# A decoder step's indexer: sequences in pairs on two row halves and two column tiles, prompt scores over four PSUM banks

## The chip, the cores and the metric

The kernel runs on one core of one Trainium2 chip. The metric is device time in microseconds (us). Before the change it is 2095.02 us, the median of three runs (2094.37 to 2096.9).

## The reference, cut to what matters

One layer of a hybrid decoder serves a prompt of 272 rows (16 meta tokens and 256) and eight samples of eight rows each, 336 rows in all, with one set of weights. A combined projection makes queries, keys and values, the indexer's queries, keys and head weights, and the conv and gate inputs. The indexer scores every key for every query row, and only the best scored keys are attended to:

```python
def index_scores(iq, iw, ik, q_pos, k_pos):
    s = jnp.einsum('bqhd,bkd->bqhk', iq, ik).astype(jnp.float32) * (IDX_DIM ** -0.5)
    s = jnp.einsum('bqhk,bqh->bqk', jax.nn.relu(s), iw.astype(jnp.float32)) * (IDX_HEADS ** -0.5)
    return jnp.where(k_pos[None, None, :] <= q_pos[None, :, None], s, -jnp.inf)
```

There are 16 indexer heads of 64 values. A sample scores 1024 keys from a paged cache (8 pages of 128) and its 8 new ones, and takes the best 256; a prompt row scores up to 272 and takes 64. Attention, a conv branch, the gated merge and the feed-forward layer follow.

## The kernel before

**Weights.** The whole kernel is a stream of weight tiles of 2048 x 128. SyncE loads a tile into one of four slots of RAW (two transfers, released by `mm_done`). ScalarE makes its high part WH (`quarter`, line 558), VectorE the rest WL (line 949). TensorE multiplies each of the 16 weight blocks three times with 320 or 336 columns of activations (`split_mm`, lines 1416 to 1418). One such unit is cut into four quarters of 12 matmuls (`x_quarter`), which can be put between other work.

**Indexer keys.** GpSimd loads 64 pages (line 423). For each sequence b, ScalarE's `pages(b)` (line 599) copies the eight pages to `ikb` with the 64 values written twice, so that a key fills 128 rows. TensorE's `keys(b)` transposes eight blocks of it, and ScalarE and VectorE copy halves of the result to `ikTa` (lines 603 and 990). There are eight such sets: seven between the units of the stage "iq" (indexer queries) and one behind "ikiw" (keys and head weights).

**Indexer queries.** ScalarE evacuates each iq unit to `iqT` (prompt) and `iqs` (samples). In `iqs` the even heads lie in rows 0 to 63 and the odd ones in rows 64 to 127, in columns of their own, with zeros elsewhere (memset, line 985). One matmul of 128 rows so gives all 16 heads x 8 query rows of one sequence.

**Order on TensorE behind the ikiw unit.** The last set of keys; two quarters of the unit qk 0 (attention queries); small transposes and products that end with `d_setup` (line 1550 and on); the two other quarters of qk 0; then, sequence by sequence, `scores(b)` (two fp32 matmuls of 512 columns into SB or TB), relu on ScalarE (line 650) and VectorE (line 1027) to `rl`, and `total(b)` (two matmuls of 512 columns with the head weights IW, 64 columns wide, added up over all eight sequences in MB). Eight small matmuls score the new keys (`n_mm`), eight more sum them. VectorE copies the sums to Ss and Ws (lines 1032 to 1035).

**Prompt scores.** A loop of 32 steps (16 heads x 2 query tiles; in each four steps two with 144 and two with 272 keys): TensorE makes the scores of one head in a bank of SB (`i % 2`), with contraction over 64 rows, even heads in rows 0 to 63 and odd ones in rows 64 to 127; ScalarE's relu writes `rp` (line 657); VectorE multiplies it by the head's weight and adds it to Sp (lines 1042 and 1045). After each eight steps TensorE does a quarter of the unit qk 1. TensorE waits for the relu two steps back, ScalarE for the addition two steps back.

**Behind the loop.** ScalarE waits for all 32 additions, makes WH of the third unit of qk, and then squares the first unit; TensorE waits for that square (`squares(0)`, in the page `psM<-sq,ones`), and goes on with the third unit.

`ikT`, the new keys, exists in rows 0 to 63; GpSimd copies it to rows 64 to 127 by a transfer (line 435) once `ik_cp` has its four counts.

Of the kernel before, what the change touches and what calls it, by code (L numbers as in the profile page):

```python
# [31 lines left out]
P = 128  # L32
# [3 lines left out]
NS = B * Q  # L36
# [7 lines left out]
NPG = PAST // PAGE  # L44
LS = PAST + Q
# [81 lines left out]
def place(persistent, transient):  # L127
# [64 lines left out]
    ("ikst", [P, B, NPG, ID], F32, ST_A, ST_IKIW),  # L192
    ("iqT", [P, H, SEQ], F32, ST_IQ, ST_INDEX), ("iqs", [P, B, H, 2, Q], F32, ST_IQ, ST_INDEX),
# [3 lines left out]
    ("ikb", [P, 2, NPG, 2, ID], F32, ST_IQ, ST_IKIW), ("ikTa", [P, B, PAST], F32, ST_IQ, ST_INDEX),  # L197
    ("rl", [P, 2, PAST], F32, ST_INDEX, ST_INDEX), ("rln", [P, NS], F32, ST_INDEX, ST_INDEX), ("rp", [P, 2, NP], F32, ST_INDEX, ST_INDEX),
# [24 lines left out]
           "ut ML esel xs L ikst Tb OH vtok xTs crt ikb SGB m8p qsz ktok v2 oh relb relx m8s vst kst ya vT kTs iktok Lp CH "  # L223
# [3 lines left out]
def layer(nc, I, O):  # L227
# [44 lines left out]
    iktok, iwtok, ikb, ikTa, rl, rln, rp = (T[x] for x in ("iktok", "iwtok", "ikb", "ikTa", "rl", "rln", "rp"))  # L272
# [12 lines left out]

    def keys_of(qt):
        return N_META + P * (qt + 1)

    with ExitStack() as ctx:
        G, TB, SB, MB = ([ctx.enter_context(nc.psum_tensor(f"ps{n}{i}", [P, 512], F32)) for i in range(2)] for n in "GTSM")  # L290

# [12 lines left out]
        pool_init, pool_zero, pt_dn = sem("pool_init"), sem("pool_zero"), sem("pt_dn")  # L304
# [4 lines left out]
        pg_ld, d_setup, d_iw, d_ikt, d_page, ik_tr = sems("pg_ld", B), sem("d_setup"), sem("d_iw"), sem("d_ikt"), sem("d_page"), sem("ik_tr")  # L309
        n_mm, d_rln, ik_dp, ik_cp = sem("n_mm"), sem("d_rln"), sem("ik_dp"), sem("ik_cp")  # L310
# [90 lines left out]
        def _(pool):  # L401
# [13 lines left out]
            pool.tensor_copy(ptab2[:].rearrange("o (g n c) -> o g n c", g=B // 2, c=2), ptab[:].rearrange("o (g c n) -> o g n c", g=B // 2, c=2)).then_inc(pt_dn, 1)  # L415
            pool.wait_ge(pt_dn, 1)
# [4 lines left out]
            for b in range(B):  # L421
                for t in range(NPG):
                    pool.dma_start(ikst[:, b:b + 1, t, :], cache_ik[bass.ds(page(b * NPG + t), 1)].rearrange("o s d -> s o d")).then_inc(pg_ld[b], 16)
                if b == 0:
                    pool.wait_ge(a_rms, 1)
                    n = XTILES[2][1]
                    pool.tensor_scalar(xs[0:n, 2, :], xtok[0:n, 2, :], stat[0:n, 10:11], None, ALU.mult).then_inc(a_xp, 1)
                    for dst, src in ((oh[:], I["c_oh"]), (relx[0:BUCKETS, :], I["rel_bias"]), (wrow[:], I["w_dw"][0]),
                                     (esel[64:64 + IH, :], I["c_esel"]), (qm[:], I["c_qm"]), (cms[:], I["c_cms"]), (cmp_[:], I["c_cmp"])):
                        pool.dma_start(dst, src).then_inc(c2_ld, 16)  # L430
                if b == 1:
# [106 lines left out]
        def _(act):  # L538
# [62 lines left out]
            def keys(b):  # L601
                act.wait_ge(ik_tr, b + 1)
                act.activation(ikTa[:, b, 0:512], TB[0][:], ACT.Copy).then_inc(d_cpA, 1)

            def iq(g):
                for s in range(4):
                    u = 4 * g + s
                    if u >= 2:
                        keys(u - 2)
# [4 lines left out]
                    act.activation(iqT[:, u, :], G[s % 2][:, 0:SEQ], ACT.Copy)  # L614
                    for r in range(2):
                        rows = slice(64 * r, 64 * r + 64)
                        ins = act.activation(iqs[rows, :, u, r, :], G[s % 2][rows, SEQ:NQ].rearrange("p (b q) -> p b q", b=B), ACT.Copy)
                    ins.then_inc(ev[s % 2], 1)
                    pages(u)
# [9 lines left out]
            keys(6)  # L629
# [10 lines left out]
            keys(7)  # L640
# [7 lines left out]
            for b in range(B):  # L648
                act.wait_ge(idx_mm, b + 1)
                act.activation(rl[:, b % 2, 0:512], (SB, TB)[b % 2][0][:], ACT.Relu).then_inc(d_rlA, 1)  # L650
# [279 lines left out]
        def _(dve):  # L930
# [54 lines left out]
            dve.memset(iqs[:], 0.0)  # L985
            dve.memset(IW[:], 0.0).then_inc(pool_zero, 1)

            def keys(b):
                dve.wait_ge(ik_tr, b + 1)
                dve.tensor_copy(ikTa[:, b, 512:PAST], TB[1][:]).then_inc(d_cpD, 1)  # L990
# [11 lines left out]
            for u in range(4 * GN["iq"]):  # L1002
                if u >= 2:
                    keys(u - 2)
                if u == 3:
                    dve.wait_ge(c2_ld, 112)
# [4 lines left out]
            for s in range(4):  # L1011
                if s == 2:
                    keys(6)
                if s == 3:
                    keys(7)
# [9 lines left out]
            for b in range(B):  # L1025
                dve.wait_ge(idx_mm, b + 1)
                dve.tensor_scalar(rl[:, b % 2, 512:PAST], (SB, TB)[b % 2][1][:], 0.0, None, ALU.max).then_inc(d_rlD, 1)
            dve.wait_ge(n_mm, 1)
            dve.tensor_scalar(rln[:], SB[0][:, 0:NS], 0.0, None, ALU.max).then_inc(d_rln, 1)
            dve.wait_ge(sum_mm, B)  # L1030
            for i in range(2):
                dve.tensor_copy(Ss[:, 512 * i:512 * i + 512], MB[i][0:NS, :])
            dve.wait_ge(sum_mm, B + 1)
            ch.link(dve.tensor_tensor(Ss[:, PAST:LS], TB[0][0:NS, 0:Q], cms[:], ALU.min))
            dve.tensor_copy(Ws[:], Ss[:]).then_inc(d_ss, 1)

            for i in range(2 * IH):
# [3 lines left out]
                if h == 0:  # L1041
                    ins = dve.tensor_scalar(Sp[:, qt, 0:nk], rp[:, i % 2, 0:nk], iwtok[:, qt, h:h + 1], None, ALU.mult)
                else:
                    dve.wait_ge(pp_acc, i if i % 2 else i - 2)
                    ins = dve.scalar_tensor_tensor(Sp[:, qt, 0:nk], rp[:, i % 2, 0:nk], iwtok[:, qt, h:h + 1], Sp[:, qt, 0:nk],
# [361 lines left out]
        def _(pe):  # L1407
# [96 lines left out]
            def keys(b):  # L1504
                pe.wait_ge(d_page, b + 1)
                if b:
                    pe.wait_ge(d_cpA, b)
                    pe.wait_ge(d_cpD, b)
                for t in range(NPG):
                    ins = tr(TB[t // 4][:, P * (t % 4):P * (t % 4) + P], ikb[:, b % 2, t, :, :].rearrange("p r d -> p (r d)"))  # L1510
                ins.then_inc(ik_tr, 1)

            for u in range(4 * GN["iq"]):
# [4 lines left out]
                if u:  # L1518
                    keys(u - 1)
                if u == 3:  # L1520
                    pe.wait_ge(c2_ld, 112)
# [20 lines left out]
            keys(B - 1)  # L1542
# [3 lines left out]
            pe.wait_ge(d_cpA, B)  # L1546
            pe.wait_ge(d_cpD, B)
# [9 lines left out]
            for r in range(2, 4):  # L1557
# [420 lines left out]
```

## Time and profile before

| | |
|---|---|
| median of three runs | 2095.02 us |
| span of the profiled execution, first to last instruction | 2085.9 us |
| TensorE busy | 2031.4 us, 97% |
| VectorE busy | 1244.2 us, 60% |
| ScalarE busy | 888.5 us, 43% |
| GpSimd busy | 165.6 us, 8% |
| mean granted TensorE clock | 0.990 |
| HBM read, written | 338.91 MB, 10.83 MB |

The execution that was profiled is known by its span. The median of the runs lies 9.1 us above it, which is what lies around the first and the last instruction. A busy TensorE is one with a matmul in flight: the recorded length of a matmul holds its way through the array, so that records overlap, and the pitch from start to start tells what one costs.

### The profile page before, as it was taken

To read this page: it belongs to the slowest core of one execution; us is meant where nothing else is said; L and a number is where in the kernel's file an instruction comes from. 1 tells how busy PE (TensorE), PEld (TensorE's weight loads), DVE (VectorE), ACT (ScalarE), POOL (GpSimd) and SP (SyncE) were. 2 spreads that over 40 slices of the span, in tenths; PEclk is the share of its full clock that TensorE was granted. 3 is DMA by queue.
4 is the path that set the end of the run, shared out by engine and by line. 5 is a ranking of instruction groups with operands and counts; after the bars stand their busy time and mean duration, and the time that the engine had idled before them with its cause. 6 is when DMAs were issued, how large, how long until landed. Compare 5 with 4: busy or idle time off the path is not lost.

```text
span 2085.9 us, 40295 instructions
## 1 busy us (share of the span) xinstructions
PE 2031.4 (97%) x14517; PEld 1935.0 (93%) x14517; DVE 1244.2 (60%) x2293; ACT 888.5 (43%) x1640; POOL 165.6 (8%) x293
## 2 busy tenths in 40 slices
PE   6999999899999999999999999999999999999997
PEld 5957989899997778999999999999999999999997
DVE  5327997566667998955655555544455554455553
ACT  6424444343334333356444545533344433344443
POOL 6300000111113220010000000000000000000012
PEclk9999999999999999999999999999999999999999
DMA  9363454477768994556555555555555555555573
GB/s 240 94 127 106 128 134 130 135 227 236 237 203 291 333 323 129 147 152 197 149 154 142 157 144 147 155 142 156 146 151 150 145 157 141 156 147 152 150 204 109
DMA packets 545493, 350.54 MB, mean 168 GB/s; under 512 B 15122, under 2 KB 524346, under 8 KB 545007
## 3 DMA queue, kind: packets, MB, share of 16 engines
q1 hardware_dynamic: 518480, 263.55, 46.9%
q0 software_dynamic: 25824, 84.55, 12.5%
q8 instruction: 69, 1.13, 0.2%
q10 hardware_dynamic: 1088, 1.05, 0.2%
q14 instruction: 32, 0.26, 0.0%
HBM read 338.91 MB, written 10.83 MB: 168 GB/s over the span
## 4 chain that ended last, share of the span: by engine, by line
PE 68%; DVE 0%; ACT 0%; DMA 0%; issue 0%; POOL 0%; POOLq 0%; DVEq 0%; ACTq 0%
PE psG L1416 21%; PE psG L1417 21%; PE psG L1418 21%; PE psS L1413 2%; PE psM L1417 1%; PE psM L1418 1%; PE psM L1416 1%; PE psT L1410 0%; DMA vst<-in_cache_v 0%; PE psM L1410 0%; DVE OL L1285 0%; PE psM L1413 0%; PE psM L1774 0%; ACT WH L558 0%; POOL out L528 0%
## 5 line engine op out<-in xcount | busy, mean ns | idle before, releaser
L949 DVE TENSOR_TENSOR WL<-RAW,WH 128x512 fp32r<-128x512 f32 (+1 forms) x996 | 674.1, 691 | 624.4 <-ACT WH L558 622.5
L558 ACT ACTIVATE WH<-RAW 128x512 fp32r<-128x512 f32 (+1 forms) x996 | 613.8, 628 | 820.9 <-PE psG L1418 761.4
L1416 PE MATMUL psG<-XH,WH 128*128 128x320 f32 (+1 forms) x2688 | 852.8, 317 | 2.5 <-DVE WL L949 2.1
L1417 PE MATMUL psG<-XL,WH 128*128 128x320 f32 (+1 forms) x2688 | 838.5, 312 | 0.0
L1418 PE MATMUL psG<-XH,WL 128*128 128x320 f32 (+1 forms) x2688 | 836.9, 311 | 0.0
L1416 PEld LDWEIGHTS psG<-XH,WH 128*128 128x128 f32 x2688 | 507.4, 189 | 32.9 <-issue 25.0
L1417 PEld LDWEIGHTS psG<-XL,WH 128*128 128x128 f32 x2688 | 507.6, 189 | 1.6 <-issue 0.2
L1418 PEld LDWEIGHTS psG<-XH,WL 128*128 128x128 f32 x2688 | 507.5, 189 | 0.0
L1416 PE MATMUL psG<-MH,WH 128*128 128x320 f32 x960 | 297.9, 310 | 0.3 <-DVE ML L1385 0.3
L1418 PE MATMUL psG<-MH,WL 128*128 128x320 f32 x960 | 296.6, 309 | 0.0
L1417 PE MATMUL psG<-ML,WH 128*128 128x320 f32 x960 | 296.6, 309 | 0.0
L1416 PEld LDWEIGHTS psG<-MH,WH 128*128 128x128 f32 x960 | 180.5, 188 | 0.5 <-issue 0.5
L1417 PEld LDWEIGHTS psG<-ML,WH 128*128 128x128 f32 x960 | 180.5, 188 | 0.0
L1418 PEld LDWEIGHTS psG<-MH,WL 128*128 128x128 f32 x960 | 180.5, 188 | 0.0
L1249 DVE SCALAR_TENSOR_TENSOR ya<-ub,wdw,ya 128x256 f32<-128x256 f32 x232 | 99.9, 478 | 0.0
L527 POOL DMA_DIRECT2D out<-ytok x16 | 11.4, 712 | 1083.8 <-ACT ytok L909 1079.7
L1410 PE MATMUL psT<-ident,kst 128*128 128x128 f32 x512 | 68.9, 278 | 0.0
L1410 PEld LDWEIGHTS psT<-ident,kst 128*128 128x128 f32 x512 | 57.9, 142 | 6.8 <-issue 6.3
L759 ACT ACTIVATE kTs<-psT 128x512 f32<-128x512 f32 x64 | 38.2, 597 | 56.5 <-PE psT L1410 56.2
L1169 DVE COPY kTs<-psT 128x512 f32<-128x512 f32 x64 | 43.9, 686 | 25.3 <-PE psT L1410 25.3
L899 ACT ACTIVATE MH<-at 128x320 f32 x44 | 20.8, 472 | 83.0 <-DVE at L1383 83.0
L467 POOL DMA_DIRECT2D kst<-in_cache_k x64 | 33.9, 530 | 175.2 <-issue 175.2
(342 smaller groups left out, 1661.3 us busy)
## 6 DMA issues: line engine op xcount, KB each, us to landing
RAW<-in_w_in SPq DMA_DIRECT2D x160, 512.0 KB, 5.2
RAW<-in_w_ffn_down SPq DMA_DIRECT2D x96, 512.0 KB, 5.1
RAW<-in_w_ffn_gate SPq DMA_DIRECT2D x88, 512.0 KB, 4.8
RAW<-in_w_ffn_up SPq DMA_DIRECT2D x88, 512.0 KB, 4.7
kst<-in_cache_k POOLq DMA_DIRECT2D x64, 512.0 KB, 4.2
vst<-in_cache_v POOLq DMA_DIRECT2D x64, 512.0 KB, 6.0
RAW<-in_w_out SPq DMA_DIRECT2D x32, 512.0 KB, 4.7
RAW<-in_w_attn_br SPq DMA_DIRECT2D x16, 512.0 KB, 5.0
```

The lines of the kernel that those rows point to most:

```text
L467: pool.dma_start(dst[:, n:n + 1, :], src[bass.ds(page(g * m + n, ptab2), 1)].rearrange("o s n -> s o n")).then_inc(landed[n], 16)
L558: act.activation(WH[:, s % 2, 4 * r:4 * r + 4, c], RAW[:, s, 4 * r:4 * r + 4, c], ACT.Copy).then_inc(hi_done, 1)
L759: act.activation(kTs[:, j % 2, 0:4, :], TB[0][:].rearrange("p (h n) -> p h n", h=4), ACT.Copy).then_inc(kc_A, 1)
L899: act.activation(MH[:, bass.ds(g * 2 + s // 2, 1), :], at2[:, s // 2:s // 2 + 1, :], ACT.Copy).then_inc(ah_dn, 1)
L949: dve.tensor_tensor(WL[:, s, k, c], RAW[:, s, k, c], WH[:, s % 2, k, c].bitcast(F32), ALU.subtract).then_inc(lo_done, 1)
L1169: dve.tensor_copy(kTs[:, j % 2, 4:8, :], TB[1][:].rearrange("p (h n) -> p h n", h=4)).then_inc(kc_D, 1)
L1249: ch.step(dve.scalar_tensor_tensor(z, x, tap, z, ALU.mult, ALU.add))
L1410: return pe.transpose(out, src, ident[0:n, 0:n])
L1413: return pe.matmul(out, lhsT, rhs, start=start, stop=stop, skip_group_check=True)
L1416: pe.matmul(out, WH[:, s % 2, k], hi, start=start, stop=False)
L1417: pe.matmul(out, WH[:, s % 2, k], lo, start=False, stop=False)
L1418: return pe.matmul(out, WL[:, s, k], hi, start=False, stop=stop)
```

## The change

- `ikst` holds the pages of sequences p and p + 4 side by side, and their transposes give keys of p in rows 0 to 63 and of p + 4 in rows 64 to 127. The copy to `ikb` is gone; there are four sets of keys (behind units 2, 4, 6 and behind ikiw) instead of eight. GpSimd loads the sequences in the order 0, 4, 1, 5, ...
- `iqs` holds each sequence's 16 heads in its own row half. ScalarE writes the heads that lie in the right half at once and the others to `iqx`; two transfers on GpSimd's queue move these to the other half. The memset is gone.
- `scores(p)`: four matmuls of 64 rows, in turn on row half 0 and row half 1, to SB and TB; two signals, one for each 512 keys. `total(p)`: four matmuls with 32 columns of weights, in turn in column tiles 0 to 31 and 32 to 63.
- Between `scores(p)` and `total(p)` stands a quarter of qk (0, 2), (0, 3), (1, 0), (1, 1). A quarter (1, 2) stands ahead of the sum of the new keys, and (1, 3) behind step 15 of the prompt loop. The two quarters that stood ahead of the first scores are gone from there.
- The first scores wait for all three transfers (`ik_dp` 48) and for `d_iw` and `d_ikt`.
- The prompt loop uses four banks, SB and TB, and four parts of `rp`; all waits are four steps back instead of two. Step 2 waits for VectorE's reading of TB[0].
- ScalarE copies the first half of the sums to Ss; VectorE copies the second half behind the `min` of the new keys.

```diff
-            for b in range(B):
+            for i in range(B):
+                b = i // 2 + PAIRS * (i % 2)
                 for t in range(NPG):
-                    pool.dma_start(ikst[:, b:b + 1, t, :], ...).then_inc(pg_ld[b], 16)
+                    pool.dma_start(ikst[:, b % PAIRS, t, i % 2:i % 2 + 1, :], ...).then_inc(pg_ld[b], 16)
...
+            pool.wait_ge(iq_cp, 2 * H)
+            pool.dma_start(iqs[0:ID, :, 1], iqx[ID:2 * ID]).then_inc(ik_dp, 16)
+            pool.dma_start(iqs[ID:2 * ID, :, 0], iqx[0:ID]).then_inc(ik_dp, 16)
             pool.wait_ge(ik_cp, 4)
             pool.dma_start(ikT[ID:2 * ID, :], ikT[0:ID, :]).then_inc(ik_dp, 16)
...
-            def pages(b):
-                act.wait_ge(pg_ld[b], 16 * NPG)
-                act.activation(ikb[:, b % 2], ikst[:, b, :, None, :].to_broadcast([P, NPG, 2, ID]), ACT.Copy).then_inc(d_page, 1)
...
+            for p in range(PAIRS):
+                for r in range(2):
+                    act.wait_ge(idx_mm, 2 * p + 1)
+                    act.activation(rl[:, r, 0:512], (SB, TB)[r][0][:], ACT.Relu).then_inc(d_rlA, 1)
+            act.wait_ge(sum_mm, PAIRS)
+            act.activation(Ss[:, 0:512], MB[0][0:NS, :], ACT.Copy).then_inc(d_rlA, 1)
...
-                if i >= 2:
-                    act.wait_ge(pp_acc, i - 1)
-                act.activation(rp[:, i % 2, 0:nk], SB[i % 2][:, 0:nk], ACT.Relu).then_inc(pp_relu, 1)
+                if i >= 4:
+                    act.wait_ge(pp_acc, i - 3)
+                act.activation(rp[:, i % 4, 0:nk], PP[i % 4][:, 0:nk], ACT.Relu).then_inc(pp_relu, 1)
...
-            for r in range(2, 4):
-                x_quarter(G0["qk"], 0, r)
...
+                if p == 0:
+                    pe.wait_ge(ik_dp, 48)
...
+                for i in range(2):
+                    for r in range(2):
+                        ins = mm((SB, TB)[r][i][:], iq_of(p + PAIRS * r), ikTa[ID * r:ID * r + ID, p, 512 * i:512 * i + 512])
+                    ins.then_inc(idx_mm, 1)
...
+                for i in range(2):
+                    for r in range(2):
+                        b = p + PAIRS * r
+                        ins = mm(MB[i][rows_of(b), :], iw_of(b), rl[:, r, 512 * i:512 * i + 512], p == 0, p == PAIRS - 1)
+                ins.then_inc(sum_mm, 1)
+
+            between = [(0, 2), (0, 3), (1, 0), (1, 1)]
+            for p in range(PAIRS):
+                scores(p)
+                x_quarter(G0["qk"], *between[p])
+                total(p)
...
+            x_quarter(G0["qk"], 1, 2)
             pe.wait_ge(d_rln, 1)
...
-                if i >= 2:
-                    pe.wait_ge(pp_relu, i - 1)
-                mm(SB[i % 2][:, 0:nk], iqT[rows, h // 2, P * qt:P * qt + P], ikT[rows, 0:nk]).then_inc(pp_mm, 1)
-                if i % 8 == 7:
-                    x_quarter(G0["qk"], 1, i // 8)
+                if i >= 4:
+                    pe.wait_ge(pp_relu, i - 3)
+                if i == 2:
+                    pe.wait_ge(d_rln, 2)
+                mm(PP[i % 4][:, 0:nk], iqT[rows, h // 2, P * qt:P * qt + P], ikT[rows, 0:nk]).then_inc(pp_mm, 1)
+                if i == 15:
+                    x_quarter(G0["qk"], 1, 3)
```

## Rows read from the trace of the kernel before

**Rows 1.** The page, part 1: engine, busy us, share of the span, instructions.
```profile
PE 2031.4 (97%) x14517; PEld 1935.0 (93%) x14517; DVE 1244.2 (60%) x2293; ACT 888.5 (43%) x1640; POOL 165.6 (8%) x293
```

**Rows 2.** Windows: stretch, its us, busy of each engine, granted clock, DMA share.
```profile
123.40:155.10 31.70, 31.70 (x82) 11.15 (x81) 5.75 (x9) 4.78 (x8) 0.00 (x0) 1.00 0.56 68
156.10:179.70 23.60, 20.24 (x102) 13.64 (x100) 13.72 (x34) 9.77 (x31) 0.00 (x0) 0.97 0.08 22
179.70:183.60 3.90, 3.80 (x13) 3.30 (x12) 3.21 (x8) 2.90 (x7) 1.51 (x2) 0.50 0.26 31
...
400.00:2080.00 1680.00, 1660.43 (x12291) 1606.67 (x12291) 983.27 (x1738) 706.15 (x1238) 103.84 (x183) 1.00 0.62 177
```

**Rows 3.** Timeline of TensorE, one key set: start, us, line, tile, shape, count.
```profile
49.98 1.04 PE L1410 MATMUL psT<-ident,ikb 128*128 128x128 f32 x8
50.77 0.39 PE L1416 MATMUL psG<-XH,WH 128*128 128x320 f32 x1
```

**Rows 4.** Timeline of TensorE, sample scores and sums (two records a matmul).
```profile
126.97 1.93 PE L1413 MATMUL psM<-rl,IW 128*64 128x512 f32 x4
128.83 1.98 PE L1413 MATMUL psS<-ikTa,iqs 128*128 128x512 f32 x4
130.75 1.93 PE L1413 MATMUL psM<-rl,IW 128*64 128x512 f32 x4
...
151.48 1.95 PE L1413 MATMUL psS<-ikT,iqs 128*128 128x8 f32 x16
...
155.13 1.05 PE L1413 MATMUL psT<-rln,IW 128*64 128x8 f32 x16
```

**Rows 5.** Timeline of TensorE, matmuls on two row halves and on four column tiles.
```profile
156.11 0.39 PE L1413 MATMUL psS<-ikT,iqT 64*128 64x144 f32 x2
...
157.00 0.90 PE L1413 MATMUL psS<-ikT,iqT 64*128 64x272 f32 x4 [0.37 <-ACT rp L657]
...
652.75 3.64 PE L1413 MATMUL psS<-vst,L 128*32 128x512 f32 x32 [0.94 <-ACT PTn L792]
```

**Rows 6.** Timeline: a relu of VectorE; where a quarter of qk 1 begins and ends.
```profile
125.36 0.69 DVE L1027 TENSOR_SCALAR rl<-psS 128x512 f32<-128x512 f32 x1 [5.04 <-PE psS L1413]
...
172.89 0.42 PE L1416 MATMUL psG<-XH,WH 128*128 128x336 f32 x1
...
174.95 0.39 PE L1413 MATMUL psS<-ikT,iqT 64*128 64x144 f32 x2
```

**Rows 7.** The copy of ikT: DMA view (KB, us to landing), issue, TensorE's last setup work.
```profile
ikT<-ikT POOLq DMA_DIRECT2D x1, 84.0 KB, 5.1
...
115.59 0.54 POOL L435 DMA_DIRECT2D ikT<-ikT  x1 [25.01 <-ACT iwT L639]
...
119.36 0.34 PE L1410 MATMUL psT<-ident,ikT 64*128 64x64 f32 x3
```

**Rows 8.** Timeline of VectorE: copy to Ws, then steps of the prompt loop.
```profile
156.72 0.69 DVE L1035 COPY Ws<-Ss 64x1032 f32<-64x1032 f32 x1
...
175.82 0.37 DVE L1045 SCALAR_TENSOR_TENSOR Sp<-rp,iwtok,Sp 128x144 f32<-128x144 f32 x1 [1.61 <-ACT rp L657]
...
176.29 0.37 DVE L1045 SCALAR_TENSOR_TENSOR Sp<-rp,iwtok,Sp 128x144 f32<-128x144 f32 x1
...
177.03 1.89 DVE L1045 SCALAR_TENSOR_TENSOR Sp<-rp,iwtok,Sp 128x272 f32<-128x272 f32 x4 [0.37 <-ACT rp L657]
```

**Rows 9.** Timeline: VectorE's last step of the loop; what lets TensorE go on.
```profile
180.31 0.50 DVE L1045 SCALAR_TENSOR_TENSOR Sp<-rp,iwtok,Sp 128x272 f32<-128x272 f32 x1 [0.20 <-ACT rp L657]
...
181.10 2.19 ACT L558 ACTIVATE WH<-RAW 128x512 fp32r<-128x512 f32 x4 [0.82 <-DVE Sp L1045]
...
183.72 1.40 PE L1413 MATMUL psM<-sq,ones 128*128 128x336 f32 x2 [0.22 <-issue]
```

**Rows 10.** Windows elsewhere: TensorE little busy, then busy at half clock.
```profile
308.00:311.20 3.20, 1.19 (x7) 1.14 (x8) 3.17 (x6) 1.89 (x2) 2.27 (x3) 1.00 0.61 158
311.20:314.60 3.40, 3.40 (x13) 3.23 (x13) 3.33 (x8) 1.39 (x5) 1.05 (x2) 0.50 1.13 348
```

More of the change, by code:

```diff
@@ L44 @@
 NPG = PAST // PAGE
+PAIRS = B // 2
 LS = PAST + Q
@@ L607, in iq @@
                     u = 4 * g + s
-                    if u >= 2:
-                        keys(u - 2)
+                    if u in KEYS_AT:
+                        keys(KEYS_AT.index(u))
                     ahead(G0["iq"] + g, s)
@@ L984, in _, with keys @@
             dve.wait_ge(x_wr, 16)
-            dve.memset(iqs[:], 0.0)
             dve.memset(IW[:], 0.0).then_inc(pool_zero, 1)
-            def keys(b):
-                dve.wait_ge(ik_tr, b + 1)
-                dve.tensor_copy(ikTa[:, b, 512:PAST], TB[1][:]).then_inc(d_cpD, 1)
+            def keys(p):
+                dve.wait_ge(ik_tr, p + 1)
+                dve.tensor_copy(ikTa[:, p, 512:PAST], TB[1][:]).then_inc(d_cpD, 1)
             def tables():
@@ L1556, in _ @@
             ins.then_inc(d_setup, 1)
-            for r in range(2, 4):
-                x_quarter(G0["qk"], 0, r)
-            def zero(out, start):
-                n = out.shape[1]
-                w = min(n, NS)
-                return mm(out, zer[:, 0:out.shape[0]], ones[:, None, 0:w].to_broadcast([P, n // w, w]), start, not start)
             def iq_of(b):
-                return iqs[:, b].rearrange("p h r q -> p (h r q)")
+                half = ID * (b // PAIRS)
+                return iqs[half:half + ID, b % PAIRS].rearrange("p r h q -> p (r h q)")
@@ L1568, in iw_of, with rows_of, scores @@
             def iw_of(b):
-                return IW[:].rearrange("p b n -> p (b n)")[:, NS * b:NS * b + NS]
-            def scores(b):
-                out = (SB, TB)[b % 2]
-                if b == 1:
+                at = NS * b + NS // 2 * (b // PAIRS)
+                return IW[:].rearrange("p b n -> p (b n)")[:, at:at + NS // 2]
+            def rows_of(b):
+                return slice(NS // 2 * (b // PAIRS), NS // 2 * (b // PAIRS) + NS // 2)
+            def scores(p):
+                if p == 0:
+                    pe.wait_ge(ik_dp, 48)
+                if p == 0:
@@ L1588, in _ @@
-            scores(0)
-            scores(1)
-            for b in range(B):
-                total(b)
-                if b + 2 < B:
-                    scores(b + 2)
-                if b == B - 2:
-                    pe.wait_ge(ik_dp, 16)
-                    for n in range(B):
-                        ins = mm(SB[0][:, Q * n:Q * n + Q], iq_of(n), ikT[:, NP + Q * n:NP + Q * n + Q])
-                    ins.then_inc(n_mm, 1)
+                for i in range(2):
+                    for r in range(2):
+                        ins = mm((SB, TB)[r][i][:], iq_of(p + PAIRS * r), ikTa[ID * r:ID * r + ID, p, 512 * i:512 * i + 512])
+                    ins.then_inc(idx_mm, 1)
@@ L1599, in _ @@
+            for n in range(B):
+                b = n // 2 + PAIRS * (n % 2)
+                rows = slice(ID * (n % 2), ID * (n % 2) + ID)
+                ins = mm(SB[n % 2][:, Q * b:Q * b + Q], iq_of(b), ikT[rows, NP + Q * b:NP + Q * b + Q])
+            ins.then_inc(n_mm, 1)
+            x_quarter(G0["qk"], 1, 2)
             pe.wait_ge(d_rln, 1)
-            for b in range(B):
-                ins = mm(TB[0][0:NS, 0:Q], iw_of(b), rln[:, Q * b:Q * b + Q], b == 0, b == B - 1)
+            for n in range(B):
+                b = n // 2 + PAIRS * (n % 2)
+                ins = mm(TB[0][rows_of(b), 0:Q], iw_of(b), rln[:, Q * b:Q * b + Q], n < 2, n >= B - 2)
```

126 lines of the change are left out of this document (59 added, 67 removed).

## The prediction

> **What bounds the kernel now.** I read the page first: TensorE is busy for 97% of the span [rows 1]. Then the windows: behind 400 us it is busy for 1660 of 1680 us, so whatever the indexer stage gives or takes, the rest only starts earlier or later; no engine or queue there works to a fixed time. The stage that changes has two parts [rows 2]. From 123.4 to 155.1 us TensorE is busy all the time with fp32 matmuls of the sample indexer, and VectorE and ScalarE for 6 and 5 us: there only less TensorE work saves time. From 156.1 to 179.7 us (prompt loop) it still shows 20 of 23.6 us, with three quarters (36 matmuls) of qk 1 inside, but each step waits for the one before on another engine. I then read both parts in order of time for the pitch of each matmul.
>
> **Key sets.** A set of eight transposes begins at 49.98 and the next weight matmul at 50.77; its record of 0.39 is 0.08 longer than the 0.31 of its neighbours [rows 3]. One set costs 0.79 + 0.08 = 0.87 us of a TensorE that never waits there; four go: **-3.5 us**. ScalarE loses the 1.06 us page copy and gains two small evacuations of each unit, beside matmuls. The pages arrive in the new order long before units 2, 4 and 6 end. One more small constant load on GpSimd delays the xT store by its issue (0.5 us), the memset that is gone gives 0.9 back; TensorE has a unit of work ahead there, so I take 0.
>
> **First scores.** Before, two quarters of qk (3.8 us) stood between the setup and the first scores and covered the transfers. Now the scores stand right behind the setup, whose last transposes start at 119.36 and are followed by the next work at 119.6, and they wait for the copy of ikT: issued at 115.59, landed 5.1 us later, at 120.7 [rows 7]. Nothing is queued on TensorE that could go first. The iqx transfers are issued about 10 us earlier, so the ikT copy ends last. **+1.2 us** (0.5 if the copy lands in 4.4; 5 if the weight loads beside it hold it up).
>
> **Sample scores and sums.** `scores` and `total` pitch 1.86 and 1.92 us [rows 4]: four passes of 0.43 us and 0.1 to 0.2 where the kind of weights changes. Two sequences cost 7.55 us. The new code needs eight matmuls, thus sixteen passes, for two sequences as well, but in pairs on separate tiles. Do they overlap? The prompt loop's first two matmuls use row halves 0 and 1: their first passes both lie inside 0.39 us from 156.11, which is one pass of 144 columns with its way through the array; so they ran side by side. On column tiles, 32 passes of 512 columns on four tiles took 3.64 us [rows 5], which is eight times 0.43 and 0.2 for the way out: all four side by side. I take full overlap: `scores(p)` 4 x 0.43 = 1.71, `total(p)` 1.71. The quarter between them takes 2.06 from start to next start [rows 6], with 0.2 of change in it, and total to scores costs 0.15 more: 5.63 us for a step, 22.5 for four, of which 4 x 1.86 is weight work that stood elsewhere. The relus: VectorE has two of 0.69 with a pitch of 0.6 [rows 6] behind the last score pass: 0.15 + 1.29 = 1.45 us, within the quarter's 1.86. So no wait; the cover has 0.4 us to spare. The new keys' 16 passes took some 1.9 us (the record group of 1.95 from 151.48) [rows 4]; in row pairs I take 1.0 (0.9 to 1.9). Then a quarter, 2.06, and the sums of the new keys, 1.0 before [rows 4], 0.6 now. First scores to prompt loop: 22.5 + 1.0 + 2.06 + 0.6 = 26.2 us.
>
> **Prompt loop.** VectorE starts later in it: `min`, a copy to Ss (0.6), the copy to Ws 0.69 [rows 8] in a row: first step 1.85 us behind the first matmul. Then with four banks nothing but VectorE is late: for four steps ScalarE needs 1.2 us, TensorE 0.7 in row pairs, VectorE 0.47 from a 144-key step to the next that adds to the same sums (175.82 to 176.29), 0.3 from there to the first 272-key one (an estimate: under 0.47, since it needn't wait for the result before it), and, for the rest of four, what the row of four steps shows: 272, 272, 144, 144 in 1.89 us, so 1.52 to the start of the last [rows 8], of which 0.47 is the 144 pair again. Together 0.3 + 1.52 = 1.8. Eight times: 14.4 us. Loop to last addition: 16.2 us (18 if each step costs 0.5). The one quarter at step 15 is hidden: VectorE then has seven steps (3.3 us) in hand. From the last addition (180.31 + 0.50) to `squares(0)` at 183.72 are 2.9 us [rows 9]: ScalarE's WH of 2.19 and the square. That chain is unchanged. Before, a quarter of qk filled it; now TensorE stands still in it, and that is what is late next. Loop and tail: 16.2 + 2.9 = 19.1 us.
>
> **The sum at full clock.** Setup end to `squares(0)`: before, 119.6 to 183.72 = 64.1 us. After, 1.2 + 26.2 + 19.1 = 46.5 us. Both hold the same six quarters, (0, 2) to (1, 3). So -17.6, and -3.5 for the keys: -21.1 us.
>
> **Clock.** Granted clock is 1.00 up to 178 us and 0.50 (1.2 GHz) from 179.7 [rows 2], where it costs the last quarter about 1.5 us. Where TensorE was little busy (1.19 of 3.2 us) the next 3.4 us ran at 0.50 though fully busy [rows 10]. The new loop has 0.7 us of array work in 1.8, and ends in 4 us without any, so I expect half clock when it goes on: 3.4 to 6.8 us of it, 1.7 to 3.4 us lost, against 0.6 lost in the same place before (the 1.5 of the quarter is already in the 64.1). I take +2.0, and +0.4 for the quarter in the loop if it too is slow. **Sum: -18.7 us.** In the profiled execution that is 2085.9 - 18.7 = 2067.2; the median stands 9.1 above the span, so 2076.3 us.
>
> **A rule that speaks against full overlap.** The rows show four column tiles side by side (3.64 us for 32 passes). The Trainium skill (TensorE: Matmul & The Clock Gate, Part 3, packing small matmuls) gives measured speedups of 2.38 for three column tiles and 3.07 for four row tiles, thus less than the count; by its ratio of 2.38 to 3 (an estimate from that page) two tiles would gain 1.6, the 16 pairs of 0.86 us would take 3.5 us more, and the time would be 2079.8. The mechanism is rival A's. A second rule, of the Trainium skill (TensorEngine Tiling, PSUM bottleneck), says that evacuation may become the limit once matmuls are packed; without the quarter between, the relus of 1.45 us would stand open four times, +5.8 us. Here the quarter covers them by 0.4 us, and the sum takes nothing for it.
>
> **Rivals.**
> A. Pairs overlap only in part at 512 columns. The 272-column pair took 0.90 us for four passes of 0.23 where a full overlap would be about 0.62 with the way out; it was released in two steps, so it is no clean witness [rows 5]. At a quarter more for each of the 16 pairs: 16 x 0.21 = 3.4 us. Time 2079.7. If one kind (row or column) doesn't overlap at all: 8 pairs x 0.86 = 6.9 us, 2083.2. That is the case that the change doesn't do what it says; both kinds, 2090.
> B. The loop costs more than VectorE's pitch: at half clock TensorE's steps take 1.4 of 1.8 us and the slow quarter (3.4 us) opens a gap of 1 us, or each step needs 0.5: +2 to +3. Time 2079.
> C. The clock comes back sooner, with none of the 2.4 us that I add for it and the 0.6 us of before gone too: -3, 2073.
> D. Slower: the transfers that the first scores now wait for land late. The 84 KB copy takes 5.1 us beside weight loads at full DMA load [rows 7]. Each us of landing above that is one us of the kernel; from 5.1 + 18.7 = 24 us on the change is a loss. For it: it shares 16 engines with weight loads that fill them; against it: the same copy in the same company took 5.1. Landing at 30 us, the time is 2095.0 + 6 = 2101.
>
> **Chances.** Forecast 0.62 (2073 to 2079); A 0.14, B 0.12, C 0.09, D 0.03. Range 2071 to 2085. The measurement tells about 0.2%, 4.2 us, from no change; all but D and A with both kinds lie beyond it on the fast side: faster 0.94, same 0.03, slower 0.03.
>
> **What would show it.** Key sets: four groups of eight `psT<-ident,ikst`. Scores: groups of eight records of 64x512 in 1.9 us with starts two by two, and a wait of about 1.2 us ahead of the first. Loop: VectorE idle under 1 us between steps, TensorE waiting. Behind it: some 4 us idle and half clock. Wrong if the 64x512 passes start one by one at 0.43, if the quarter is followed by a wait for VectorE's relu, or if TensorE in the qk stage loses time that it did not lose before.

## The result and the profile after

The changed kernel takes 2070.17 us, the median of four runs (2067.42 to 2070.53), beside 2094.69 us for the kernel before in four runs (2089.24 to 2096.9). The ratio is 0.9883 with a 95% interval from 0.9862 to 0.9905: **24.5 us faster**. The forecast was 18.7 us faster, at 2076.3 us, with a range down to 2071; the time lies 0.8 us below that range. The sign was right, the size was not. The time around the span is not 9.1 us, as the table of the kernel before has it, but 1.5: the profiled execution of the changed kernel took 2070.0 us at a span of 2068.5.

The first part of the page of the changed kernel answers to [rows 1]; its span is 2068.5 us:

```profile
PE 2013.7 (97%) x14485; PEld 1926.7 (93%) x14485; DVE 1238.0 (60%) x2288; ACT 879.4 (43%) x1645; POOL 167.6 (8%) x296
```

Windows of the changed kernel (stretch, its us, busy of PE, PEld, DVE, ACT, POOL, granted clock, DMA share, GB/s), beside [rows 2]. In order: the wait for the ikT copy, the first scores, the prompt loop up to its quarter, the quarter, the rest of the loop, its tail, the stretch behind it.

```profile
117.40:120.00 2.60, 0.01 (x1) 0.00 (x0) 2.17 (x6) 0.97 (x4) 1.32 (x2) 0.95 1.14 264
119.70:123.20 3.50, 3.16 (x8) 1.19 (x8) 0.00 (x0) 1.04 (x2) 1.86 (x4) 0.51 1.00 189
147.80:153.90 6.10, 6.09 (x48) 4.07 (x48) 5.00 (x13) 3.96 (x13) 0.00 (x0) 1.00 0.50 52
153.90:157.30 3.40, 3.40 (x10) 2.70 (x11) 2.56 (x7) 1.09 (x4) 0.00 (x0) 0.50 0.51 130
157.30:164.10 6.80, 6.46 (x37) 4.22 (x36) 4.59 (x12) 4.42 (x15) 0.00 (x0) 1.00 0.65 174
164.10:169.00 4.90, 0.05 (x1) 0.08 (x1) 3.84 (x10) 3.13 (x8) 1.51 (x2) 0.50 0.16 20
169.00:174.40 5.40, 5.40 (x18) 4.95 (x19) 5.27 (x15) 3.97 (x9) 0.00 (x0) 0.50 0.87 324
```

The timeline of TensorE in the changed kernel (start, us, line, operation, shape, count, idle time before and what ended it) answers to [rows 4, 5, 9]. The rows of 64x512 come in pairs, one for each row half:

```profile
117.07 0.34 PE L1417 MATMUL psT<-ident,ikT 64*128 64x64 f32 x3
120.04 1.22 PE L1420 MATMUL psS<-ikTa,iqs 64*128 64x512 f32 x1 [2.63 <-DMA ikT<-ikT]
120.04 1.22 PE L1420 MATMUL psT<-ikTa,iqs 64*128 64x512 f32 x1
...
125.53 1.91 PE L1420 MATMUL psM<-rl,IW 128*32 128x512 f32 x8
127.37 0.69 PE L1420 MATMUL psS<-ikTa,iqs 64*128 64x512 f32 x1
127.38 0.69 PE L1420 MATMUL psT<-ikTa,iqs 64*128 64x512 f32 x1
127.91 0.59 PE L1420 MATMUL psS<-ikTa,iqs 64*128 64x512 f32 x1
127.91 0.59 PE L1420 MATMUL psT<-ikTa,iqs 64*128 64x512 f32 x1
128.34 0.59 PE L1420 MATMUL psS<-ikTa,iqs 64*128 64x512 f32 x1
128.34 0.59 PE L1420 MATMUL psT<-ikTa,iqs 64*128 64x512 f32 x1
...
131.34 1.91 PE L1420 MATMUL psM<-rl,IW 128*32 128x512 f32 x8
...
168.95 1.46 PE L1420 MATMUL psM<-sq,ones 128*128 128x336 f32 x2 [5.17 <-ACT sq L674]
...
389.95 3.33 PE L1420 MATMUL psM<-QK,qsz 128*32 128x64 f32 x128 [0.47 <-DVE oT L1136]
393.21 1.09 PE L1417 MATMUL psT<-ident,kst 128*128 128x128 f32 x8
```

ScalarE ahead of the copy of ikT, and VectorE in the prompt loop of the changed kernel, which answers to [rows 8]:

```profile
110.83 2.19 ACT L569 ACTIVATE WH<-RAW 128x512 fp32r<-128x512 f32 x4 [5.85 <-DMA RAW<-in_w_in]
112.93 0.48 ACT L641 ACTIVATE ikT<-psM 64x168 f32<-64x168 f32 x2
...
150.96 5.81 DVE L1052 SCALAR_TENSOR_TENSOR Sp<-rp,iwtok,Sp 128x272 f32<-128x272 f32 x13
158.88 7.16 DVE L1052 SCALAR_TENSOR_TENSOR Sp<-rp,iwtok,Sp 128x144 f32<-128x144 f32 x16 [2.11 <-ACT rp L665]
```

The reader is to see four things. Two passes of 512 columns start within 10 ns of each other (127.91), and the next two 0.43 us later (128.34): full overlap. TensorE stands 2.63 us ahead of the first scores, and these then run at 1.2 GHz. VectorE has one gap in the loop, of 2.11 us, behind the quarter that ran at half clock. And the run of 128 small matmuls at 389.95 has no gap in it; it takes 3.33 us, most of it at half clock, where the same run at full clock takes 1.99 further below.

### The profile page after: what moved, and what is told of

Read it like the earlier page. It is cut to its first block, busy times and chain, and to the rows that moved or that the text cites. A ratio compares the mean times of both kernels' runs of the same rounds, so it can differ in the third digit from the quotient of the medians.

```text
span 2068.5 us, 40223 instructions
## 1 busy us (share of the span) xinstructions
PE 2013.7 (97%) x14485; PEld 1926.7 (93%) x14485; DVE 1238.0 (60%) x2288; ACT 879.4 (43%) x1645; POOL 167.6 (8%) x296
## 4 chain that ended last, share of the span: by engine, by line
PE 69%; DVE 0%; ACT 0%; DMA 0%; issue 0%; POOL 0%; POOLq 0%; DVEq 0%; ACTq 0%
PE psG L1423 21%; PE psG L1424 21%; PE psG L1425 21%; PE psS L1420 2%; PE psM L1423 1%; PE psM L1424 1%; PE psM L1425 1%; PE psT L1417 0%; PE psM L1417 0%; DMA vst<-in_cache_v 0%; DVE OL L1292 0%; PE psM L1420 0%; PE psM L1785 0%; ACT WH L569 0%; ACT utok L786 0%
## 5 line engine op out<-in xcount | busy, mean ns | idle before, releaser
L907 ACT ACTIVATE MH<-at 128x320 f32 x44 | 20.8, 472 | 83.0 <-DVE at L1390 83.0
```

The costliest lines, as they stand in the source:

```text
L907: act.activation(MH[:, bass.ds(g * 2 + s // 2, 1), :], at2[:, s // 2:s // 2 + 1, :], ACT.Copy).then_inc(ah_dn, 1)
```

## The experiments

Each ratio is to runs of the kernel before that were made along with that version, with its 95% interval. The intervals reach 0.0013 to 0.0027 to either side (3 to 6 us), so that a difference of a few us between two versions rests on stretches of their traces, and the medians only have to agree with it.

### The kernel before, once more

The time after lay 1.5 us above its span, where the prediction had put 9.1. So the kernel before ran again with no edit.

> The kernel before, unchanged, for a second profile and the spread of its runs. Its profiled execution (span 2085.9) stands 9.1 us below the median of its runs, while the changed kernel's (span 2068.5) stands 1.5 us below its own. If the time around the span is a constant (my prediction took 9.1), spans here will be 9 us below the times. If it is some 1.5 us and the executions themselves differ (my theory now), span and time differ by 1.5 in each run, and the runs spread from 2087 to 2097 with stalls or half-clock stretches that come and go.

2095.13 us (12 runs, 2092.96 to 2098.77), ratio 1.0004 (0.9989 to 1.0019). The profiled execution took 2095.08 us with a span of 2093.6: 1.5 us around it. Its windows over the prompt loop, which answer to [rows 2]:

```profile
158.40:161.40 3.00, 2.32 (x14) 1.38 (x13) 2.65 (x7) 1.56 (x5) 0.00 (x0) 1.00 0.48 131
161.40:175.00 13.60, 12.82 (x42) 9.56 (x42) 5.22 (x13) 3.52 (x11) 0.00 (x0) 0.50 0.03 8
175.00:185.30 10.30, 8.42 (x46) 5.90 (x45) 5.33 (x13) 3.94 (x14) 0.00 (x0) 1.00 0.00 1
185.30:192.00 6.70, 6.48 (x19) 4.64 (x18) 5.19 (x12) 4.92 (x12) 1.51 (x2) 0.50 0.32 76
```

In the execution on which the prediction rests the clock stayed at 1.00 from 156 to 178 us; here 13.6 us of the same loop ran at 0.50, and from the loop's first matmul to `squares(0)` it is 32.3 us instead of 27.6. The setup (all that stands before the last `ident,ikT` transposes) is another 2.3 us longer, with 6.9 us at half clock instead of 3.4. The first profiled execution of before was thus a quick one: 2085.9 + 1.5 = 2087.4 us. A third profile with this loop, of the next experiment, agrees with the second: 13.5 us at 0.50 and 32.4 us. Of the 49 runs of the kernel before that were made along with the experiments nine lie under 2090 us, the lowest at 2087.19; the medians of the three groups are 2094.8 to 2095.7.

### The run of small matmuls moved in the instruction stream

In both profiles of before, TensorE stands 4 us inside the run of 128 small matmuls of stage attention, for nothing that the profile shows, then runs on at half clock; in the changed kernel it doesn't. Nothing there was edited, so the rows below of the unchanged kernel ask for a cause.

```profile
409.76 1.88 PE L1413 MATMUL psM<-QK,qsz 128*32 128x64 f32 x119 [0.47 <-DVE oT L1129]
415.55 0.48 PE L1413 MATMUL psM<-QK,qsz 128*32 128x64 f32 x9 [3.92 <-issue]
415.96 1.97 PE L1410 MATMUL psT<-ident,kst 128*128 128x128 f32 x8
```

In the first profile of before one 16 KB packet of the instruction queue is read between 406.2 and 406.3 us, inside the gap that ends at 408.51. The edit puts waits that are already met at the start of TensorE's program, in before 128 of them and in after 104, so that everything behind them lies elsewhere in its instruction stream:

```diff
+            for _ in range(128):          # in after: 104
+                pe.wait_ge(pool_init, 1)
```

> The kernel before, with 128 waits (already met) at TensorE's start, where it stands idle for 14 us anyway; every later TensorE instruction lies 8 KB further on in its stream. Theory: the 4 us in which TensorE waits for nothing at 404.5 us, with a 16 KB block of the instruction queue read in it, is an instruction fetch that falls due right behind a burst of 64 tiny matmuls, and it takes 2 to 3.4 us more by half clock behind it. Then the gap goes and the time falls by 4 to 7 us against the kernel before (2094.7 to 2088 to 2091). Rival: the gap is something of the data (a load, a semaphore): no change.

> The changed kernel with 104 waits (already met) at TensorE's start, which put the burst of 64 tiny matmuls at 390 us about where it lay in the kernel before, against the 16 KB blocks in which instructions are read. Theory: 5 us of the saving are nothing but that the change made TensorE's stream shorter by some 74 instructions ahead of the burst: the gap of 4 us and its half clock come back, +5 to +6.5 us (2075 to 2077). Rival: the gap went for another reason: no change (2070).

Before with the waits: 2091.06 us, ratio 0.9975 (0.9962 to 0.9988), 4.6 us less than the runs of before made along with it. The gap is gone:

```profile
411.25 1.99 PE L1413 MATMUL psM<-QK,qsz 128*32 128x64 f32 x128 [0.48 <-DVE oT L1129]
413.17 1.09 PE L1410 MATMUL psT<-ident,kst 128*128 128x128 f32 x8
```

After with the waits: 2079.0 us, ratio 0.9929 (0.9907 to 0.995), 8.8 us more than without, and more than the 5 to 6.5 expected. The gap is back, one matmul behind the run:

```profile
391.63 0.33 PE L1417 MATMUL psT<-ident,kst 128*128 128x128 f32 x1
395.97 1.75 PE L1417 MATMUL psT<-ident,kst 128*128 128x128 f32 x7 [4.01 <-issue]
```

From the start of the run to the second set of `kst` transposes are 11.2 us with the gap (before) and 4.71 in before with the waits; 6.06 in after and 10.4 in after with the waits. So the gap itself accounts for 4.4 of the 8.8 us; the rest goes with stretches at half clock that after doesn't have or has shorter, around the first scores (6.9 us at 0.55) and at 614 us (13.7 us at 0.51), and no run shows whether the waits cause them. About 5 us of the gain come from where the run lies in the stream, and the change moved it by having fewer instructions ahead. That the position makes and unmakes the gap is shown. That the gap is instruction fetch stays an inference, though a consistent one: in each of the four profiles with a gap (both of before, before on four banks further below, after with the waits) one packet of the instruction queue is read inside it, and in after and in before with the waits none is read during the run.

### Sums without column tiles, scores over all rows

```diff
-  ins = mm(MB[i][rows_of(b), :], iw_of(b), rl[...], p == 0, p == PAIRS - 1)
+  ins = mm(MB[i][0:NS, :], IW[...][:, NS*b:NS*b+NS], rl[...], p == 0 and r == 0, p == PAIRS - 1 and r == 1)
```

> The changed kernel with its sums in one column tile of 64 (IW windows of 64 columns as before, into all 64 rows of MB), so that no two of them can run side by side. If the two 32-column tiles overlap in full, total(p) takes 3.45 instead of 1.75 us: +6.9 us (2077). If they overlap not at all, as in the rival of the prediction, +0.

2078.58 us, ratio 0.992 (0.9896 to 0.9945).

```profile
127.00 3.65 PE L1420 MATMUL psM<-rl,IW 128*64 128x512 f32 x8
130.58 0.69 PE L1420 MATMUL psS<-ikTa,iqs 64*128 64x512 f32 x1
...
134.55 3.65 PE L1420 MATMUL psM<-rl,IW 128*64 128x512 f32 x8
```

Where after needs 1.84 us from the sum to the next scores it needs 3.58, and from the start of the first sum to the scores of the new keys, behind the last, 26.22 us against 19.26: 6.96 more, as expected (6.9).

The scores over all 128 rows (this kernel leaves out the separate scores of a pair's two sequences):

```diff
-  ins = mm((SB, TB)[r][i][:], iq_of(p + PAIRS * r), ikTa[ID * r:ID * r + ID, p, ...])
+  ins = mm((SB, TB)[r][i][:], iqs[:, p].rearrange("p r h q -> p (r h q)"), ikTa[:, p, ...])
```

> The changed kernel with the sample scores contracted over all 128 rows of iqs and ikTa, so that each sums the scores of both sequences of its pair (the separate scores of the two are left out); the count, width and order of the matmuls stay. If the row halves overlap in full, scores(p) takes 3.45 instead of 1.72 us: +6.9 us (2077), less up to 1 where the first scores ran at half clock. Rival: no overlap at 512 columns, +0.

2075.83 us, ratio 0.9904 (0.9879 to 0.9928).

```profile
126.49 1.91 PE L1420 MATMUL psM<-rl,IW 128*32 128x512 f32 x8
128.33 1.13 PE L1420 MATMUL psS<-ikTa,iqs 128*128 128x512 f32 x2
...
131.01 1.02 PE L1420 MATMUL psT<-ikTa,iqs 128*128 128x512 f32 x2
...
133.82 1.91 PE L1420 MATMUL psM<-rl,IW 128*32 128x512 f32 x8
```

The step is 7.33 us instead of 5.81, 1.52 more, and the first scores give 1.48 more: 6.05 in all, somewhat less than the 6.9 expected. Both kinds of pairs overlap, as the starts of the rows above show, and each kind is worth 6 to 7 us. Rival A is out.

### The prompt loop: two banks in after, four banks in before

```diff
-                if i >= 4:
-                    pe.wait_ge(pp_relu, i - 3)
-                mm(PP[i % 4][:, 0:nk], ...)
+                if i >= 2:
+                    pe.wait_ge(pp_relu, i - 1)
+                mm(SB[i % 2][:, 0:nk], ...)
```

(and ScalarE and VectorE likewise)

> The changed kernel with its prompt loop back on two banks and two parts of rp (waits two steps back); quarters stay where the change put them. Theory: VectorE sets the pace of the loop either way (0.45 us a step with four banks, some 0.51 with two), so it costs 32 x 0.06 = 2 us, and 1 to 2 more since at the quarter behind step 15 VectorE has one step in hand instead of four: +2 to +4 us (2072 to 2074). Rival: the four banks are what shortened the loop, from 24 us to 17: +7 (2077).

2078.52 us, ratio 0.9927 (0.99 to 0.9954); from the loop's first matmul to `squares(0)` 27.7 us against 20.8. The expectation of +2 to +4 us was wrong, and its rival of +7 came nearer. VectorE in it:

```profile
154.22 2.09 DVE L1052 SCALAR_TENSOR_TENSOR Sp<-rp,iwtok,Sp 128x272 f32<-128x272 f32 x4 [0.89 <-ACT rp L665]
157.20 2.09 DVE L1052 SCALAR_TENSOR_TENSOR Sp<-rp,iwtok,Sp 128x272 f32<-128x272 f32 x4 [0.89 <-ACT rp L665]
...
164.20 0.84 DVE L1052 SCALAR_TENSOR_TENSOR Sp<-rp,iwtok,Sp 128x144 f32<-128x144 f32 x2 [2.90 <-ACT rp L665]
...
167.53 1.89 DVE L1052 SCALAR_TENSOR_TENSOR Sp<-rp,iwtok,Sp 128x272 f32<-128x272 f32 x4 [0.23 <-ACT rp L665]
```

At full clock (167.53) two banks leave VectorE idle for 0.23 us every four steps; at half clock (154 to 160 us) for 0.89, and for 2.90 behind the slow quarter. The reverse, four banks alone in the kernel before, its four quarters left where they were:

```diff
-                if i >= 2:
-                    pe.wait_ge(pp_relu, i - 1)
-                mm(SB[i % 2][:, 0:nk], ...)
+                if i >= 4:
+                    pe.wait_ge(pp_relu, i - 3)
+                if i == 2:
+                    pe.wait_ge(d_ss, 1)
+                mm((SB[0], SB[1], TB[0], TB[1])[i % 4][:, 0:nk], ...)
```

> The kernel before with one part of the change alone: four banks and four parts of rp in the prompt loop, all waits four steps back; its four quarters stay in the loop. Theory, from the loop on two banks in the changed kernel (+7 us): the banks are worth that much here too, since VectorE goes on while TensorE does a quarter: -6 to -8 us, 2087 to 2089. Rival: with four quarters in the loop TensorE itself has 8 + 8 us of work at full clock and far more at half, and the gain is under 3.

2085.61 us, ratio 0.995 (0.9932 to 0.9968), some 9.9 us below before, where 6 to 8 were expected. Loop to `squares(0)`: 23.4 us, against 32.3 and 27.6 in the two profiles of before. VectorE there:

```profile
167.10 3.63 DVE L1045 SCALAR_TENSOR_TENSOR Sp<-rp,iwtok,Sp 128x144 f32<-128x144 f32 x8 [2.69 <-ACT rp L657]
171.54 3.63 DVE L1045 SCALAR_TENSOR_TENSOR Sp<-rp,iwtok,Sp 128x144 f32<-128x144 f32 x8 [0.81 <-ACT rp L657]
175.99 3.63 DVE L1045 SCALAR_TENSOR_TENSOR Sp<-rp,iwtok,Sp 128x144 f32<-128x144 f32 x8 [0.82 <-ACT rp L657]
```

A full-clock quarter leaves VectorE 0.8 us open, a half-clock one 2.7. The banks come out at 8.4 us (taken from the changed kernel) and 9.9 (put into the one before), against 8.4 and 5.7 between the medians for the two kinds of pairs and 7.1 for the order within the step below: with intervals of 3 to 6 us these runs don't rank them. The banks are worth most where the clock is low, and the two go together: of the four profiles with a loop on two banks three ran 10 us or more of it at 0.50, and of the nine with four banks none more than 3.4 us up to TensorE's last step. Why is not shown.

### The cover ahead of the first scores and the last quarter of the loop

Quarter (0, 2) ahead of the first scores again, the other four moved up by one:

```diff
+            x_quarter(G0["qk"], 0, 2)
...
-            between = [(0, 2), (0, 3), (1, 0), (1, 1)]
+            between = [(0, 3), (1, 0), (1, 1), (1, 2)]
...
-            x_quarter(G0["qk"], 1, 2)
```

> The changed kernel with one quarter, (0, 2), back ahead of the first scores, the four between the steps moved up by one, none ahead of the sum of the new keys. Theory: the quarter covers 2.0 of the 2.6 us wait for the copy of ikT, the half-clock stretch that begins there (119.7 to 123.2 us) and costs 1.5 goes too, and VectorE's work on the new keys is open for 0.6: -3 us (2067). Rival: the copy isn't what decides, or the clock falls all the same: -1.4 or less.

2067.23 us, ratio 0.9872 (0.9848 to 0.9896), 2.9 us below the changed kernel, as expected. The wait is 0.49 us, and the first scores run at full clock: 3.98 us from them to the first sum instead of 5.49.

```profile
121.24 0.69 PE L1420 MATMUL psS<-ikTa,iqs 64*128 64x512 f32 x1 [0.49 <-DMA ikT<-ikT]
121.25 0.69 PE L1420 MATMUL psT<-ikTa,iqs 64*128 64x512 f32 x1
...
155.45 7.17 DVE L1052 SCALAR_TENSOR_TENSOR Sp<-rp,iwtok,Sp 128x144 f32<-128x144 f32 x16 [0.59 <-ACT rp L665]
```

The last row is VectorE behind the quarter at step 15: here, and in after with the waits, that quarter ran at full clock, and it opens 0.6 us instead of 2.11. So 1.5 us of this profile's lead over that of after are not due to the cover.

Quarter (1, 3) behind step 31 instead of step 15:

```diff
-                if i == 15:
+                if i == 31:
```

> The changed kernel with the quarter (1, 3) behind step 31 instead of step 15. Theory: at step 15 it runs at half clock and VectorE stands still for 2.1 us; behind the loop it fits into the 5.2 us in which TensorE waits for ScalarE's square. So -2.1 us (2068), and the wait behind the loop shrinks by 3.5 at half clock. Rival: the loop without any full work loses the clock for longer and the units behind pay for it: 0 to +2.

2066.99 us, ratio 0.987 (0.9846 to 0.9895), 3.2 us below the changed kernel. VectorE runs through without a gap, and loop to `squares(0)` is 18.55 us instead of 20.76:

```profile
152.76 12.89 DVE L1052 SCALAR_TENSOR_TENSOR Sp<-rp,iwtok,Sp 128x272 f32<-128x272 f32 x29
```

### The quarter behind the sums instead of ahead of them

```diff
                 scores(p)
-                x_quarter(G0["qk"], *between[p])
                 total(p)
+                x_quarter(G0["qk"], *between[p])
```

> The changed kernel with the quarter of each step behind total(p) instead of ahead of it, so that nothing stands between the scores and the sums that need their relus. Theory: VectorE's two relus (0.15 + 1.29 us behind the last score pass) stand open in each of four steps: +1.5 x 4 = +6 us (2076). Rival: the relus of the first banks start one us earlier, and less is open: +3.

2077.29 us, ratio 0.9906 (0.9888 to 0.9923), 7.1 us above the changed kernel. TensorE waits for VectorE's relus in each step:

```profile
126.23 1.91 PE L1420 MATMUL psM<-rl,IW 128*32 128x512 f32 x8 [1.49 <-DVE rl L1033]
...
133.61 1.91 PE L1420 MATMUL psM<-rl,IW 128*32 128x512 f32 x8 [1.48 <-DVE rl L1033]
```

The step is 7.37 us, 1.56 more. So the order within the step is worth 6.4 us from the first scores to the loop (34.51 against 28.15).

### The version that the runs point to

The cover, the last quarter behind step 31, and the WH and WL of the third unit of qk made by ScalarE and VectorE during step 1 of the sample indexer instead of behind the loop:

```diff
+                if p == 1:
+                    ahead(G0["qk"], 0)      # ScalarE and VectorE, behind the relus
```

(and unit 0 of the later loop over qk leaves it out)

> The changed kernel with what the runs so far point to: quarter (0, 2) ahead of the first scores and the four between moved up by one (alone: -3), (1, 3) behind step 31 (alone: -3), and the WH and WL of the third unit of qk made by ScalarE and VectorE behind their relus of step 1, where both stand idle, instead of behind the loop. Theory: the 2.9 us from the last addition to squares(0) shrink to some 0.6 of ScalarE's square, but the quarter at half clock stands there now and ends 2 us behind the last addition, so -1 from that; in sum -6 to -7 us against the changed kernel: 2064. Rival: the three share one idle stretch and one clock stretch, and no more than the better of them stays: 2067.

2060.97 us (2059.61 to 2063.68), ratio 0.9832 (0.9816 to 0.9848), below the changed kernel's interval, 3 us lower than expected and the fastest of all.

```profile
161.56 0.45 ACT L676 ACTIVATE sq<-psG 128x336 f32<-128x336 f32 x1 [1.32 <-DVE Sp L1059]
...
162.65 0.72 PE L1430 MATMUL psM<-sq,ones 128*128 128x336 f32 x2
```

The square follows VectorE's last addition at once instead of 2.4 us behind it (168.42 against 166.04), and TensorE goes from the quarter into `squares(0)` without the 5.17 us of after. It also keeps its clock: the 5.4 us behind `squares(0)` ran at 1.00 (162.6 to 168.0), where after has 0.50, and from there to the run of small matmuls it is 218.35 us instead of 221.00. The third part was not run alone; the other two gave 2.9 and 3.2 us, and 3.1 of the 9.2 are left for it and for what the three do together.

## Why the prediction was wrong

By stages, in us (the first stage is the setup, from the span's start to the last transposes; the second, for example, is 31.12 = 148.19 - 117.07 in after and 36.75 = 156.11 - 119.36 in before):

| stage | predicted | after less first profile of before | after less second profile of before |
|---|---|---|---|
| up to the last setup transposes | -3.5 | -2.3 | -4.6 |
| to the loop's first matmul | -9.1 | -5.6 | -5.6 |
| to `squares(0)` | -8.1 | -6.9 | -11.6 |
| to the run of small matmuls | +2.0 | +2.1 | +2.0 |
| to the second `kst` set | 0 | -5.2 | -5.1 |
| rest | 0 | +0.5 | -0.2 |
| sum | -18.7 | -17.4 | -25.1 |

**The step that failed** is the closing one: "the median stands 9.1 above the span, so 2076.3 us." The surroundings of a span are 1.5 us in the profiled execution of after, of before run again, and of every experiment. The other 7.6 us were the distance between a quick execution and a typical one. With 1.5 in its place the same sum gives 2068.7 us, 1.5 below the measured time.

**The sum of the span was right by luck.** Against the first profile, on which it rests, the forecast of the span is 1.3 us off (2067.2 for 2068.5). But it missed +1.2 in the setup, +3.5 ahead of the loop and +1.2 in it, and most of that was made good by 5.2 us at the run of small matmuls, which no step had.

**What the quick execution hid.** The false step reaches into the term of the loop: the 27.6 us from first matmul to `squares(0)` held the full clock up to 178 us, and "0.6 lost in the same place before" was read from that one execution. The two other profiles with that loop (32.3 and 32.4 us) lose 4.7 us more there, and the changed kernel doesn't: with four banks the loop hangs on VectorE, which keeps its 0.45 us a step (rows at 150.96 and 158.88) while TensorE does the quarter at half clock, until its banks are used up. In all profiles of four banks with one quarter in the loop it is 19.2 us where that quarter ran at full clock and 20.7 to 20.8 where it ran at half: 1.5 us for the clock, where two banks pay 4.7. No row of after has the loop's own matmuls at half clock. The 7.6 us are thus no constant that before and after share: of the 7.7 us between the two spans of before 4.7 lie in the loop and 2.3 in the setup.

**The clock as a cost of before.** The prediction counted half clock as something that the change adds (+2.4 us). The two-bank loop paid for it twice, by slower quarters and by steps that wait for TensorE; both runs on the loop's banks show it (+6.9 in the loop with two banks in after; -8.9 with four in before against the second profile, -4.2 against the quick first one). The prediction had priced that as VectorE's pace at full clock only.

**The run of small matmuls.** No step of the prediction has it; -5.1 us. In the profile of before the 4 us at "issue" stood in plain view at 408.51, and the text said that behind 400 us "the rest only starts earlier or later".

**First scores.** "+1.2 us" was 2.6. The copy took 5.8 us instead of 5.1, and it was issued 2.85 us ahead of the last transposes where [rows 7] have 3.77: the transposes come 2.3 us sooner than before, the copy only 1.4. ScalarE evacuates ikT behind the WH of the next weight tile, and that began at 110.83, when the tile had landed (5.85 us of waiting for its transfer), so that `ikT<-psM` began 1.7 us behind the end of TensorE's products (112.93 against 111.19) where before it was 0.6 (114.30 against 113.66). The profiles of the versions of the changed kernel below show that wait too, 5.7 to 6.1 us. The stop then brought 3.4 us at half clock to the first scores, another 1.5. Both go with a quarter ahead of them.

**Steps of the samples.** 5.81 us for 5.63: sums, scores and quarter took 1.84, 1.92 and 2.05, where the prediction had 1.71, 1.71 and 2.06 with 0.15 for the change between kinds. From first scores to loop 28.15 for 26.2, of which 1.5 is the clock. The new keys' scores took 1.00 us from start to next start (144.79 to 145.79), as said; the 1.06 of their record holds the way out. The last sums took 0.35 for 0.6.

**A rule that spoke against full overlap.** Rows of after show pairs at a pitch of 0.43 us, and the two runs without pairs cost 6.96 and 6.05 us, where twice the passes would cost 6.9. The time that the prediction drew from the ratio of 2.38 for three tiles in the Trainium skill (TensorE: Matmul & The Clock Gate, Part 3, packing small matmuls), a gain of 1.6 for two, isn't borne out here for fp32 passes of 512 columns; three tiles were not run. The relus without cover cost 1.56 us a step where [rows 6] gave 1.45; with the rule of the Trainium skill that evacuation may become the limit (TensorEngine Tiling, PSUM bottleneck) these rows agree, already at two tiles.

**Prompt loop.** 0.448 us a step for VectorE and 2.9 us of tail, both as said. "The one quarter at step 15 is hidden" was wrong: at half clock it opened 2.11 us, twice what rival B had, and 0.6 even at full clock. Half clock behind the loop cost 2.7 us of 5.4, inside the 1.7 to 3.4; the version with all three moves, without that half clock, is 2.65 us shorter there.

Rival C didn't come, and D's copy landed 0.7 us late and no more. Against the typical execution the misses are -1.1 in the setup, +3.5 ahead of the loop, -3.5 in it, -5.1 at the run of small matmuls and -0.2 behind it: together -6.4 us in these two profiles, and -5.8 between the medians.

**What stays open.** Why one execution keeps the full clock through the two-bank loop and another doesn't, and whether the loop on four banks keeps it because of the banks. The rows show the level and what TensorE did before (2.32 us busy of 3.0 ahead of 161.4), and the same matmuls in the quick execution kept 1.00. Whether and why TensorE waits for the packet of the instruction queue in this run is open too; nor was it tried whether the gap in the run of small matmuls can be removed in another way than by moving it. No run undoes the key sets alone: the last setup transposes start at 119.4 to 123.0 us in the four profiles with eight sets and at 116.7 to 118.9 in the nine with four, so the 3.5 us are neither confirmed nor refuted to better than 2 us.

## What to carry to other kernels

Hold the profiled execution's own time against the median before a sum is built on it: if they differ by more than the few us around the span, the profile shows another execution than the typical one, and the stretch that differs is likely the one with waits between engines. A loop in which each step waits for TensorE pays for half clock with every step, so deeper buffering is worth more than its stalls at full clock say. A transfer that loses its cover costs the wait and then the clock of what follows; one block of independent work ahead of it, one moved behind the loop and the next operands made early, gave back 9 us together here.

## What the runs showed of the hardware that was not expected

- A run of 128 matmuls of 64 columns can stop for 3.9 to 4.2 us at "issue", in it or right behind it (3.97 before 408.51, 3.92 before 415.55, 4.19 in before on four banks, 4.01 before 395.97 with the waits), according to where it lies in TensorE's stream: with the waits ahead of it the time changed by -4.6 us (before) and +8.8 us (after, of which 4.4 at the run).
- Executions of the kernel before spread from 2087.2 to 2102.8 us; its two profiles, 7.7 us apart, differ in the stretches at half clock.
- After 2.6 us without work TensorE ran the next 3.5 us at 0.51 (119.7 to 123.2); after 0.49 us without work it ran on at full clock (the run with the cover, 1.00 from 121.2 to 125.2).
- Pairs of fp32 passes on two row halves and on two column tiles both ran at twice the rate: starts 0 to 10 ns apart on the row halves, and eight passes of 512 columns in 1.91 us on the column tiles (3.65 us without them).
- A half-clock stretch cost the loop on two banks 4.7 us and the loop on four banks 1.5 us (one quarter in it).
